# Branch gates and branch products by token instead of by channel in a two-layer fp32 block kernel

## The chip, the cores and the metric

The kernel runs on one core of a Trainium2 chip. The metric is device time in microseconds (us), the median of several executions; lower is better. Engines are TensorE (PE; its weight loads are shown apart as PEld), VectorE (DVE), ScalarE (ACT), GpSimd (POOL) and SyncE (SP), which issues the weight transfers.

## The reference

Two layers over 256 tokens of width 1024, all in float32. The change lies in the first layer's merge of three branches:

```python
h = rmsnorm(x, g_mix)
proj = h @ w_in                      # holds among others br_gate, 3 * 1024 columns
y_fox, y_sc, y_dn                    # three branches, 512 channels each
ys = jnp.stack([y_fox, y_sc, y_dn], axis=2)
gates = jax.nn.sigmoid(br_gate).reshape(bsz, seq, N_BRANCH, D_MODEL)
merged = jnp.sum(jnp.einsum('bsnc,ncd->bsnd', ys, w_branch) * gates, axis=2)
x = x + merged @ w_o
```

y_fox is an attention with forget gates, y_sc a gated short convolution, y_dn a gated delta rule in chunks of 64 tokens. A feed-forward part, and a second layer, follow; the change doesn't touch them.

## The kernel before

**Products in three parts.** Every weight matrix arrives in units of 128 x 2048 numbers (1 MB). Each unit is split in a high part (`whi`, rounded by ACT, L891, 3 slots) and a low part (`low`, by DVE, L1299, 5 slots), and the activations likewise (`hhi`, `hlo` in `hboth`; `ahi`, `alo`). A product is high x high, high x low and low x high, summed in PSUM. `mm(u, part)` issues half of unit u; part 0 ends with `half_done`, part 1 with `unit_done`.

**Kinds of units.** In C and B units the weights are stationary and 256 tokens stream past: the result has channels on the partitions. C units (1024 x 256 weights) issue 24 matmuls of 256 columns a half, in lines 2009, 2010 and 2015, and fill one bank, 4 or 5 in turn. B units (512 x 512 weights) do the same with bank 4 in part 0 and bank 5 in part 1, or banks 2g and 2g + 1 for the last branch. In T and D units the activations are stationary and 512 weight columns stream: the result has tokens on the partitions, 12 matmuls of 512 columns a half, in lines 2041, 2043 and 2056. Two T units with k0 = 0 and 4 accumulate in the same two banks, one bank per tile of 128 tokens.

**The order of the work.** One list, `order`, gives the order in which all engines walk through the steps; each engine executes its share of each step. The front has 38 units, numbered 0 to 37, so halves 0 to 75. `steps_at` puts the small steps of the attention and of the delta rule (`dn_...`) behind given halves. What reads a unit's result is held back in `held` and comes behind the next unit's part 0 (`flush`). At `mm(u, 0)` ACT makes `whi` of unit u + 2, as soon as unit u - 1 is done, and at `mm(u, 1)` DVE makes `low` of unit u + 2.

**The merge.** Units 20, 21, 23, 24, 26, 27, 29, 30 and 32 to 35 are the twelve gate units, 22, 25, 28, 31, 36 and 37 the branch units. ACT's `gate` (L1029) takes one bank through Sigmoid into `gates`; DVE's `merge` multiplies a bank of branch products with it (L1688) and, from the second branch on, adds (L1697). For the last branch ACT rounds the merged sum (L1081) and DVE takes the low part (`merge_lo`, L1706); the four w_o units (kind D, banks 0 to 3) follow, 256 rows each. Steps of the delta rule that the prediction names: `dn_tok`, `dn_decay` and `dn_kk` behind half 45, `dn_y` (level mask in L1621) behind 57, `dn_sum(0)` behind 65, `dn_sum(1)` and `dn_out(0)` behind 66, `dn_out(1)` behind 69. `dn_sum` on ACT sums squares (L879) and takes a Sqrt (L1065); `dn_out` rounds (L1075).

**Semaphores of the banks.** `c4`, `c5`, `g0` and `g1` count how often banks 4, 5, 0 and 1, and 2 and 3 were freed. A unit with `first` waits in part 0 for the first and in part 1 for the second name of its `free` list.

Of the kernel before, what the change touches and what calls it, by code (L numbers as in the profile page):

```python
# [6 lines left out]
P = 128  # L7
# [17 lines left out]
def build(nc, a, shapes, place):  # L25

    T, D = shapes["x"][1:]
    TT = T // P
# [41 lines left out]
    def unit_c(w, act, needs):  # L70
        before = [u for u in units if u["kind"] in "CB" or u.get("banks") == (4, 5)]
        bank = 5 if before and before[-1]["kind"] == "C" and before[-1]["bank"] == 4 else 4
        return add("C", w, act, needs, [f"c{bank}"], bank=bank)
# [3 lines left out]

    def unit_b(w, act, k0, needs, bank, groups):
        return add("B", w, act, needs, groups, bank=bank, k0=k0)
# [73 lines left out]
    def weave(fill, mixed):  # L153


        pending = []
        halves_ = [(u, part, then) for u, *then in fill for part in range(2)]
        scale, credit, done = len(halves_) / sum(n for n, _ in mixed), 0.0, 0

        def put(u, part, then):  # L160
            order.append(("mm", u, part))
            if part == 0 and (units[u]["kind"] == "B" or held and held[0][0] == "merge"):

                flush()
            elif part == 1 and then and then[0][0] == "merge":
                flush()
                order.append(then[0])
                held.extend(then[1:])
            elif part == 0:
                pending.append(1)  # L170
            else:
                if pending:
                    flush()
                    pending.clear()
                held.extend(then)

        if held:
            put(*halves_[0])
            flush()
            pending.clear()  # L180
            done = 1
        for n, s in mixed:
            credit += n * scale
            while credit > 0.999 and done < len(halves_):
                put(*halves_[done])
                done += 1
                credit -= 1
            order.append(s)
            if pending:
                flush()  # L190
                pending.clear()
        for h in halves_[done:]:
            put(*h)
        flush()

    def attention(which):

        for g in range(8):
            if 1 <= g < 7:
                yield (1, ("att_norm", which, g - 1))  # L200
            if g < 6:
                yield (1.0 if g else 1, ("att_scores", which, g))
            if 1 <= g < 7:
                yield (1, ("att_turn", which, g - 1))
            if g >= 2:
                yield (1.5 if g == 7 else 0, ("att_values", which, g - 2))

# [37 lines left out]
    gate_unit = {}  # L245
# [26 lines left out]
    gate(1)  # L272
    gate(0)
    branch(0, 0, "fox_lo")
    gate(2)
    gate(3)
    branch(0, 1, "fox_lo")
    gate(4)
    gate(5)
    branch(1, 0, "sc_lo")  # L280
    gate(6)
    gate(7)
    branch(1, 1, "sc_lo")
    gate(11)
    gate(10)
    gate(8)
    gate(9)
# [43 lines left out]
    for at, (u, *then) in enumerate(front):  # L331
        order.append(("mm", u, 0))
        flush()
        for s in steps_at.get(2 * at, ()):
            step(*s)
        order.append(("mm", u, 1))
        if units[u]["kind"] == "B":
            order.append(then[0])
            held.append(then[1])
        else:  # L340
            held.extend(then)
        if then and then[0][:2] == ("merge", NB - 1):
            g = then[0][2]
            if g:
                held.append(("merge_lo", 1))
            held.append(("merge_lo", 2 * g))
        for s in steps_at.get(2 * at + 1, ()):
            step(*s)
    flush()
    step("merge_lo", 3)  # L350
# [205 lines left out]
    with ctx:  # L556
# [79 lines left out]
        gates = tiles(view(3072, 6144))  # L636
# [27 lines left out]
        mg = gates[:, 0:KD, :]  # L664
# [194 lines left out]
        def _(act):  # L859
# [167 lines left out]
            def gate(e, u):  # L1027
                act.wait_ge(sem("unit_done"), u + 1)
                act.activation(gates[:, 2 * e:2 * e + 2, :], tiles(ps[:, units[u]["bank"], :]), ACT.Sigmoid)\  # L1029
                   .then_inc(took(u)[0], 1)  # L1030
# [46 lines left out]
            def merge(n_, g, b, u):  # L1077
                if n_ == NB - 1:
                    s = slice(4 * g + 2 * b, 4 * g + 2 * b + 2)
                    act.wait_ge(sem("merged"), 2 * g + b + 1)  # L1080
                    act.activation(hhi[:, s, :], mg[:, s, :], ACT.Copy).then_inc(sem("merged_hi"), 1)  # L1081
# [166 lines left out]
            def dn_unit():  # L1248
# [11 lines left out]
                         dn_sol=dn_sol, dn_out=dn_out, merge=merge, ple_gate=ple_gate, ple_p=ple_p,  # L1260
# [13 lines left out]
        def _(dve):  # L1274
# [406 lines left out]
            def merge(n_, g, b, u):  # L1681
                done = sem("half_done") if b == 0 else sem("unit_done")
                dve.wait_ge(done, u + 1)
                dve.wait_ge(*took(gate_unit[4 * n_ + 2 * g + b]))
                s = 4 * g + 2 * b
                merged = mg[:, s:s + 2, :]
                gate_ = gates[:, KD * n_ + s:KD * n_ + s + 2, :]
                ins = dve.tensor_tensor(gate_, tiles(ps[:, units[u]["bank"] + b, :]), gate_, ALU.mult)  # L1688
                if n_ < NB - 1:
                    own(ins, f"c{4 + b}", units[u]["free"][b][1] + 1)  # L1690
                elif b == 1:
# [8 lines left out]
                else:  # L1700
                    own(ins, "merged", 2 * g + b + 1)

            def merge_lo(i):
                dve.wait_ge(sem("merged_hi"), i + 1)
                s = slice(2 * i, 2 * i + 2)
                dve.tensor_tensor(hlo[:, s, :], mg[:, s, :], hhi[:, s, :].bitcast(F32), ALU.subtract)\  # L1706
                   .then_inc(sem("merged_lo"), 1)
# [169 lines left out]
            def gla_turn(b):  # L1877
# [8 lines left out]
                for t in range(TT):  # L1886
                    dve.wait_ge(sem("gla_hi"), 2 * b + t + 1)
                    for i in range(4):
# [15 lines left out]
                         dn_new=dn_new, dn_state=dn_state, dn_out=dn_out, merge=merge, merge_lo=merge_lo, resid=resid, up=up,  # L1904
# [12 lines left out]
        def _(pe):  # L1917
            def mm(u, part):
# [40 lines left out]
                if w["kind"] in "CB":  # L1959
                    nk, width = (KD, 256) if w["kind"] == "C" else (4, 512)  # L1960
# [451 lines left out]
            parts = dict(mm=mm, norm_first=norm_first, norm_wide=norm_wide, small=small, small_turn=small_turn, fox_turn=fox_turn, fox_cum=fox_cum,  # L2412
# [17 lines left out]
def laid_out(v, np):  # L2430
# [16 lines left out]
    def cut(w, *widths):  # L2447
# [8 lines left out]
        w_gate=units(gate, D, 256), w_small=by_tile(np.concatenate([f, b_a], axis=1)),  # L2456
# [52 lines left out]
```

## Time and profile before

| | |
|---|---|
| median of 3 times | 1131.43 us (1129.44 to 1131.69) |
| span of the profiled execution | 1127.7 us, 17514 instructions |
| around the span (median less span) | 3.7 us |
| PE busy | 1100.3 us, 98% |
| PE weight loads busy | 973.8 us, 86% |
| DVE busy | 767.3 us, 68% |
| ACT busy | 556.2 us, 49% |
| mean granted TensorE clock | 0.993 |

Busy time of PE is pipelined time: its ends are modelled, so the distance from one start to the next is what counts. The profiled execution has no time of its own beside its span; the times come from other executions.

### The profile page before, as it was taken

The page shows a single profiled execution, that of the slowest core. Times are in us where ns is not written, and L with a number is a line of the kernel's source. Part 1 is how long each engine was busy: PE and PEld are TensorE (multiplying, and loading weights), DVE is VectorE, ACT ScalarE, POOL GpSimd, SP SyncE. Part 2 cuts the span into 40 slices and gives each one's busy share as a digit, 9 for nine tenths or more (in the row PEclk, how much of TensorE's full clock was granted, in tenths as well). Part 3 has the DMA queues.
Part 4 walks back from the last instruction along what each step waited for, and adds up shares of the span by engine and source line. Part 5 has one row for each costly group of instructions (what it writes and reads, how often), then busy time and mean ns, then how long its engine had stood idle before and what let it go on. Part 6 is the DMA issues. An engine that isn't in the chain of part 4 may idle for free.

```text
span 1127.7 us, 17514 instructions
## 1 busy us (share of the span) xinstructions
PE 1100.3 (98%) x7442; PEld 973.8 (86%) x7442; DVE 767.3 (68%) x937; ACT 556.2 (49%) x664; POOL 36.4 (3%) x98
## 2 busy tenths in 40 slices
PE   9989999999999999999998999999999999999997
PEld 8888998997989999998797888888888888888886
DVE  5486788554668998787677575556667866656555
ACT  6466564333535443445665454444455665444443
POOL 6000000000000000000003200000000000000000
PEclk9998999999999999999999999999999999999999
DMA  8542443333355555554453355555534435555551
GB/s 306 181 156 75 150 150 116 111 116 110 130 175 194 187 187 187 187 187 167 169 180 134 129 174 190 194 196 198 191 119 174 153 115 187 184 190 187 187 187 56
DMA packets 27455, 185.07 MB, mean 164 GB/s; under 512 B 3169, under 2 KB 3681, under 8 KB 5618
## 3 DMA queue, kind: packets, MB, share of 16 engines
q1 hardware_dynamic: 26208, 182.46, 45.9%
q10 hardware_dynamic: 1170, 1.49, 0.4%
q8 instruction: 59, 0.97, 0.3%
q14 instruction: 18, 0.15, 0.1%
HBM read 182.89 MB, written 1.05 MB: 163 GB/s over the span
## 4 chain that ended last, share of the span: by engine, by line
PE 89%; DVE 7%; ACT 2%; issue 1%; POOL 0%; DVEq 0%; ACTq 0%; POOLq 0%
PE ps L2041 12%; PE ps L2056 12%; PE ps L2043 12%; PE ps L1971 10%; PE ps L2009 9%; PE ps L2015 9%; PE ps L2010 9%; PE ps L1977 5%; DVE low L1299 2%; DVE arena L1466 1%; PE ps L2073 1%; PE ps L1991 1%; PE ps L2375 1%; PE ps L2237 1%; PE ps L2143 0%
## 5 line engine op out<-in xcount | busy, mean ns | idle before, releaser
L891 ACT ACTIVATE whi<-raw 128x2048 fp32r<-128x2048 f32 x170 | 324.3, 1913 | 333.1 <-PE ps L2056 165.8
L1299 DVE TENSOR_TENSOR low<-raw,whi 128x2048 fp32r<-128x2048 f32 x170 | 389.2, 2293 | 40.3 <-ACT whi L891 37.4
L2009 PE MATMUL ps<-hboth,whi 128*128 128x256 f32 x880 | 221.0, 289 | 3.3 <-ACT conv L980 3.3
L2010 PE MATMUL ps<-hboth,whi 128*128 128x256 f32 x880 | 217.0, 284 | 0.0
L2009 PEld LDWEIGHTS ps<-hboth,whi 128*128 128x128 f32 x880 | 169.4, 192 | 7.9 <-ACT whi L891 3.6
L2010 PEld LDWEIGHTS ps<-hboth,whi 128*128 128x128 f32 x880 | 169.7, 193 | 0.7 <-issue 0.2
L2041 PE MATMUL ps<-whi,ahi 128*128 128x512 f32 x416 | 164.2, 395 | 2.8 <-issue 1.9
L2043 PE MATMUL ps<-whi,alo 128*128 128x512 f32 x416 | 162.8, 391 | 0.0
L1971 PE MATMUL ps<-hboth,whi 128*128 128x512 f32 x512 | 128.1, 392 | 0.0
L2015 PE MATMUL ps<-hboth,low 128*128 128x256 f32 x880 | 124.2, 284 | 0.5 <-DVE low L1299 0.5
L2056 PE MATMUL ps<-low,ahi 128*128 128x512 f32 x416 | 119.7, 389 | 0.0
L2015 PEld LDWEIGHTS ps<-hboth,low 128*128 128x128 f32 x880 | 114.3, 193 | 0.7 <-DVE low L1299 0.7
L1971 PEld LDWEIGHTS ps<-hboth,whi 128*128 128x128 f32 x512 | 93.7, 188 | 18.5 <-issue 0.7
L2041 PEld LDWEIGHTS ps<-whi,ahi 128*128 128x128 f32 x416 | 78.6, 189 | 18.8 <-issue 4.0
L2056 PEld LDWEIGHTS ps<-low,ahi 128*128 128x128 f32 x416 | 78.1, 188 | 16.4
L2043 PEld LDWEIGHTS ps<-whi,alo 128*128 128x128 f32 x416 | 78.6, 189 | 14.9
L1977 PEld LDWEIGHTS ps<-hboth,low 128*128 128x128 f32 x512 | 69.8, 190 | 5.0
L2041 PE MATMUL ps<-whi,hboth 128*128 128x512 f32 x186 | 73.7, 396 | 0.0
L2043 PE MATMUL ps<-whi,hboth 128*128 128x512 f32 x186 | 72.5, 390 | 0.0
L1977 PE MATMUL ps<-hboth,low 128*128 128x256 f32 x512 | 71.4, 282 | 0.0
L1801 DVE TENSOR_TENSOR cy<-cy,ps 128x512 f32<-128x512 f32 x32 | 22.0, 687 | 70.0 <-ACT cy L1149 70.0
L1808 DVE TENSOR_TENSOR alo<-cy,ahi 128x512 fp32r<-128x512 f32 x32 | 22.2, 692 | 51.7 <-ACT ahi L1156 51.7
(376 smaller groups left out, 1216.1 us busy)
## 6 DMA issues: line engine op xcount, KB each, us to landing
raw<-in_ffn_up SPq DMA_DIRECT2D x32, 1024.0 KB, 4.8
raw<-in_ffn_down SPq DMA_DIRECT2D x32, 1024.0 KB, 4.9
raw<-in_w_up SPq DMA_DIRECT2D x22, 1024.0 KB, 4.9
raw<-in_w_gate SPq DMA_DIRECT2D x12, 1024.0 KB, 4.9
raw<-in_w_down SPq DMA_DIRECT2D x11, 1024.0 KB, 4.9
raw<-in_w_dn SPq DMA_DIRECT2D x6, 1024.0 KB, 4.9
raw<-in_w_sc SPq DMA_DIRECT2D x6, 1024.0 KB, 4.8
raw<-in_w_branch SPq DMA_DIRECT2D x6, 1024.0 KB, 4.8
```

What stands on the lines that cost most here:

```text
L891: act.activation(whi[:, u % SPLIT, :], raw[:, u % RAW, :], ACT.Copy).then_inc(sem("hi_done"), 1)
L1299: dve.tensor_tensor(wlo[:, u % RAW, :], raw[:, u % RAW, :], whi[:, u % SPLIT, :].bitcast(F32), ALU.subtract).then_inc(sem("lo_done"), 1)
L1801: own(dve.tensor_tensor(y, y, both[:, :, 0, :], ALU.add), *took_name(u))
L1808: dve.tensor_tensor(alo[:, s, :], cy[:, i % 2, :, :], ahi[:, s, :].bitcast(F32), ALU.subtract)\
L1971: pe.matmul(out, whi[:, s, at:at + P], hboth[:, k, :, :].rearrange("p a t -> p (a t)"), start=k == 0, stop=False, skip_group_check=True)
L1977: ins = pe.matmul(ps[:, w["bank"] + ct, 0:T], low[:, at:at + P], hhi[:, k, :], start=False, stop=k == KD - 1, skip_group_check=True)
L2009: pe.matmul(out, wh, hi[:, k0 + k, :], start=opens and k == 0, stop=False, skip_group_check=True)
L2010: pe.matmul(out, wh, lo[:, k0 + k, :], start=False, stop=False, skip_group_check=True)
L2015: ins = pe.matmul(out, low[:, at:at + P], hi[:, k0 + k, :], start=False, stop=k == nk - 1, skip_group_check=True)
L2041: pe.matmul(ps[:, bank, :], hi[:, k0 + k, part * P:(part + 1) * P], wh, start=w["first"] and k == 0, stop=False, skip_group_check=True)
L2043: pe.matmul(ps[:, bank, :], lo[:, k0 + k, part * P:(part + 1) * P], wh, start=False, stop=False, skip_group_check=True)
L2056: ins = pe.matmul(ps[:, bank, :], hi[:, k0 + k, part * P:(part + 1) * P], low[:, at:at + 512], start=False, stop=w["last"] and k == nk - 1 ...
```

## The change

The twelve gate units become T units of 512 x 512 weights, two (k0 = 0 and 4) for each pair of branch n and half g of the 1024 channels; the six branch units become T units too. Gates, branch products and the merged sum so have tokens on the partitions. A gate's Sigmoid is issued right behind its second unit, no longer held back, once for each tile of 128 tokens. `merge` keeps its place and its operations. The merged sum is transposed on PE in 16 pieces of 128 x 128 (`merge_turn`) into banks 4 to 7, from where ACT rounds and DVE takes the low part; `merge_turn(0)` stands ahead of the first w_o unit, `merge_turn(1)` behind it. Gates 8 to 11 come in the order (2, 1), (2, 0).

```diff
     def branch(n, g, need):
-        bank, groups = (4, ["c4", "c5"]) if n < NB - 1 else (2 * g, [f"g{g}"])
-        u = unit_b(a["w_branch"][2 * n + g], "a", BT * n, [(need, 2)], bank, groups)
+        banks, groups = ((4, 5), ["c4", "c5"]) if n < NB - 1 else ((2 * g, 2 * g + 1), [f"g{g}"])
+        u = add("T", a["w_branch"][2 * n + g], "a", [(need, 2)], groups, banks=banks, k0=BT * n, first=True, last=True)
         front.append((u, ("merge", n, g, 0, u), ("merge", n, g, 1, u)))
...
-    def gate(e):
-        u = unit_c(a["w_gate"][e], "h", h_ready)
-        gate_unit[e] = u
-        front.append((u, ("gate", e, u)))
+    def gate(n, g):
+        for half in range(2):
+            u = unit_t(a["w_gate"][2 * NB * half + 2 * n + g], half)
+            front.append((u,) if half == 0 else (u, ("gate", n, g, 0, u), ("gate", n, g, 1, u)))
+        gate_freed[n, g] = [after("c4"), after("c5")]
...
-    gate(11)
-    gate(10)
-    gate(8)
-    gate(9)
+    gate(2, 1)
+    gate(2, 0)
     branch(2, 0, "dn_lo")
     branch(2, 1, "dn_lo")
...
         order.append(("mm", u, 1))
-        if units[u]["kind"] == "B":
+        if then and then[0][0] == "gate":
+            order.extend(then)
+        elif then and then[0][0] == "merge":
             order.append(then[0])
             held.append(then[1])
...
+        if then and then[0] == ("merge", NB - 1, 1, 0, u):
+            step("merge_turn", 0)
     us = [unit_d(a["w_o"][i], "h", 2 * i, i == 0, i == 3, [("merged_lo", i + 1)]) for i in range(4)]
-    for u in us[:3]:
+    product(us[0])
+    step("merge_turn", 1)
+    for u in us[1:3]:
         product(u)
...
+            def gate(n_, g, t, u):
+                act.wait_ge(sem("half_done") if t == 0 else sem("unit_done"), u + 1)
+                act.activation(gates[:, n_, t, 512 * g:512 * (g + 1)], ps[:, 4 + t, :], ACT.Sigmoid)\
+                   .then_inc(sem(gate_freed[n_, g][t][0]), 1)
...
+            def merge_turn(g):
+                for pair in (2 * g, 2 * g + 1):
+                    act.wait_ge(sem("merge_turned"), pair + 1)
+                    act.activation(hhi[:, 2 * pair:2 * pair + 2, :], tiles(ps[:, 4 + pair, :]), ACT.Copy)\
+                       .then_inc(sem("merged_hi"), 1)
...
+            def merge_turn(g):
+                for pair in (2 * g, 2 * g + 1):
+                    dve.wait_ge(sem("merged_hi"), pair + 1)
+                    s = slice(2 * pair, 2 * pair + 2)
+                    dve.tensor_tensor(hlo[:, s, :], tiles(ps[:, 4 + pair, :]), hhi[:, s, :].bitcast(F32), ALU.subtract)\
+                       .then_inc(sem("merged_lo"), 1)
...
+            def merge_turn(g):
+                pe.wait_ge(sem("merged"), 2 * (g + 1))
+                for pair in (2 * g, 2 * g + 1):
+                    for k in (2 * pair, 2 * pair + 1):
+                        for t in range(TT):
+                            at = (k % 2) * T + t * P
+                            ins = pe.transpose(ps[:, 4 + pair, at:at + P], mg[:, t, k * P:(k + 1) * P], ident[:, :])
+                    ins.then_inc(sem("merge_turned"), 1)
...
-        w_gate=units(gate, D, 256), w_small=by_tile(np.concatenate([f, b_a], axis=1)),
+        w_gate=units(gate, 512, 512), w_small=by_tile(np.concatenate([f, b_a], axis=1)),
```

## Rows read from the trace of the kernel before

**Rows 1.** The page: busy time by engine, and the chain's shares.

```profile
PE 1100.3 (98%) x7442; PEld 973.8 (86%) x7442; DVE 767.3 (68%) x937; ACT 556.2 (49%) x664; POOL 36.4 (3%) x98
...
PE 89%; DVE 7%; ACT 2%; issue 1%; POOL 0%; DVEq 0%; ACTq 0%; POOLq 0%
```

**Rows 2.** Chain, last branch halves and first w_o: start us, us, what.

```profile
300.70 0.96 PE ps L2015 x8
...
312.22 0.96 PE ps L2015 x8
313.18 0.23 PE ps L2041
```

**Rows 3.** Chain, fox units at the kernel's start.

```profile
16.07 0.91 PE ps L2056 x4
...
35.11 0.91 PE ps L2056 x4
```

**Rows 4.** Windows: stretch, length, busy by engine (instructions), clock, DMA share, GB/s.

```profile
16.07:37.83 21.76, 21.76 (x98) 18.02 (x97) 11.73 (x10) 11.14 (x10) 6.14 (x28) 1.00 0.68 250
...
296.00:313.00 17.00, 17.00 (x144) 17.00 (x143) 13.58 (x13) 8.27 (x8) 0.00 (x0) 1.00 0.53 186
```

**Rows 5.** Timeline of PE: first and ninth or seventeenth matmul after a step.

```profile
278.11 0.39 PE L2009 MATMUL ps<-hboth,whi 128*128 128x256 f32 x1
...
280.13 1.12 PE L2015 MATMUL ps<-hboth,low 128*128 128x256 f32 x8
...
871.29 0.50 PE L2041 MATMUL ps<-whi,hboth 128*128 128x512 f32 x1
...
873.24 1.07 PE L2056 MATMUL ps<-low,hboth 128*128 128x512 f32 x4
```

**Rows 6.** Timeline of PE and DVE around half 46.

```profile
183.07 0.39 PE L2009 MATMUL ps<-hboth,whi 128*128 128x256 f32 x1
...
186.91 0.68 DVE L1688 TENSOR_TENSOR arena<-ps,arena 128x512 f32<-128x512 f32 x1
```

**Rows 7.** Timeline of ACT, DVE and PE around halves 56 and 57.

```profile
224.90 1.92 ACT L891 ACTIVATE whi<-raw 128x2048 fp32r<-128x2048 f32 x1 [4.83 <-PE ps L2015]
...
230.50 0.42 DVE L1621 TENSOR_TENSOR arena<-arena,packs 128x256 f32<-128x256 f32 x1
...
231.29 0.68 PE L2237 MATMUL ps<-arena 64*64 64x64 f32 x16
```

**Rows 8.** Timeline of ACT, and PE's half 67, from half 64 to 68.

```profile
275.61 0.60 ACT L1029 ACTIVATE arena<-ps 128x512 f32<-128x512 f32 x1
286.18 0.28 ACT L879 ACTIVATE cy<-ps 128x128 f32<-128x128 f32 x1 [9.97 <-PE ps L2294]
...
287.34 1.28 ACT L1065 ACT_TABLE_LOAD   x1
...
291.18 0.63 ACT L1075 ACTIVATE ahi<-arena 128x512 fp32r<-128x512 f32 x1 [1.70 <-DVE arena L1674]
...
286.48 0.36 PE L2009 MATMUL ps<-hboth,whi 128*128 128x256 f32 x1
```

**Rows 9.** Groups of ACT, table loads: busy us, mean ns, idle before.

```profile
L1029 ACT ACT_TABLE_LOAD x4 | 5.1, 1283 | 0.1
L1065 ACT ACT_TABLE_LOAD x2 | 2.6, 1283 | 0.0
```

**Rows 10.** Timeline of PE: eight transposes and the half after them.

```profile
164.80 1.03 PE L2194 MATMUL ps<-ident,arena 128*128 128x128 f32 x8
165.59 0.36 PE L2009 MATMUL ps<-hboth,whi 128*128 128x256 f32 x1
```

**Rows 11.** Waits of PE, 0 to 335 us: us, times, longest.

```profile
PE ps L2293 <- DVE arena L1644: 1.8, 2, 0.9
...
PE ps L2280 <- DVE xs L1653: 0.8, 1, 0.8
```

More of the change, by code:

```diff
@@ L70, in unit_c @@
     def unit_c(w, act, needs):
-        before = [u for u in units if u["kind"] in "CB" or u.get("banks") == (4, 5)]
+        before = [u for u in units if u["kind"] == "C" or u.get("banks") == (4, 5)]
         bank = 5 if before and before[-1]["kind"] == "C" and before[-1]["bank"] == 4 else 4
@@ L76, in unit_w @@
         return add("C", w, act, needs, ["c4" if bank == 4 else "c5"], bank=bank, wide=True)
-    def unit_b(w, act, k0, needs, bank, groups):
-        return add("B", w, act, needs, groups, bank=bank, k0=k0)
     def unit_t(w, half):
@@ L151, in flush @@
         held.clear()
[L153 to L206, printed above, removed]
     step("first_root", 0)
@@ L271, in build @@
     sc(1, 0)
-    gate(1)
-    gate(0)
+    gate(0, 0)
     branch(0, 0, "fox_lo")
-    gate(2)
-    gate(3)
+    gate(0, 1)
     branch(0, 1, "fox_lo")
-    gate(4)
-    gate(5)
+    gate(1, 0)
     branch(1, 0, "sc_lo")
-    gate(6)
-    gate(7)
+    gate(1, 1)
     branch(1, 1, "sc_lo")
-    gate(11)
-    gate(10)
-    gate(8)
-    gate(9)
+    gate(2, 1)
+    gate(2, 0)
     branch(2, 0, "dn_lo")
@@ L635, in build @@
         kcT = dnT[:, 2 * DH:3 * DH, :]
-        gates = tiles(view(3072, 6144))
+        gates = view(3072, 3 * TT * D).rearrange("p (n t d) -> p n t d", n=NB, t=TT)
         fqkv = view(3072, 3072).rearrange("p (t n) -> p t n", t=TT)
@@ L663, in build @@
         EG = [by(xs[:, 1, 512:1024], DH), S]
-        mg = gates[:, 0:KD, :]
+        mg = gates[:, 0]
         idle = flat[1][:, 0:P]
@@ L1025, in z @@
                    .then_inc(took(u)[0], 1)
[L1027 to L1030, printed above, removed]
+            def gate(n_, g, t, u):
+                act.wait_ge(sem("half_done") if t == 0 else sem("unit_done"), u + 1)
+                act.activation(gates[:, n_, t, 512 * g:512 * (g + 1)], ps[:, 4 + t, :], ACT.Sigmoid)\
+                   .then_inc(sem(gate_freed[n_, g][t][0]), 1)
             def dn_cum():
@@ L1259, in _ @@
                          gate=gate, dn_cum=dn_cum, dn_decay=dn_decay, dn_x0=dn_x0, dn_y=dn_y,
-                         dn_sol=dn_sol, dn_out=dn_out, merge=merge, ple_gate=ple_gate, ple_p=ple_p,
+                         dn_sol=dn_sol, dn_out=dn_out, merge_turn=merge_turn, ple_gate=ple_gate, ple_p=ple_p,
                          ab_qk=ab_qk, ab_v=ab_v, lam=lam, pool_mm=pool_mm,
@@ L1679, in dn_out, with merge @@
                 own(dve.tensor_tensor(alo[s], dnout, ahi[s].bitcast(F32), ALU.subtract), "dn_lo", t + 1)
[L1681 to L1688, printed above, removed]
+            def merge(n_, g, t, u):
+                dve.wait_ge(sem("half_done") if t == 0 else sem("unit_done"), u + 1)
+                dve.wait_ge(sem(gate_freed[n_, g][t][0]), gate_freed[n_, g][t][1])
+                s = slice(512 * g, 512 * (g + 1))
+                merged, gate_ = mg[:, t, s], gates[:, n_, t, s]
+                ins = dve.tensor_tensor(gate_, ps[:, units[u]["banks"][t], :], gate_, ALU.mult)
                 if n_ < NB - 1:
-                    own(ins, f"c{4 + b}", units[u]["free"][b][1] + 1)
-                elif b == 1:
+                    own(ins, f"c{4 + t}", units[u]["free"][t][1] + 1)
+                elif t == 1:
                     own(ins, f"g{g}", units[u]["free"][0][1] + 1)
@@ L1700, in merge @@
                 else:
[L1701 to L1707, printed above, removed]
+                    own(ins, "merged", 2 * g + t + 1)
+            def merge_turn(g):
[4 more added lines that the diff above has]
+                       .then_inc(sem("merged_lo"), 1)
             def added(xt, banks, t, u):
@@ L1903, in _ @@
                          dn_pre=dn_pre, dn_decay=dn_decay, dn_kk=dn_kk, dn_x0=dn_x0, dn_y=dn_y, dn_z=dn_z, dn_sol=dn_sol,
-                         dn_new=dn_new, dn_state=dn_state, dn_out=dn_out, merge=merge, merge_lo=merge_lo, resid=resid, up=up,
+                         dn_new=dn_new, dn_state=dn_state, dn_out=dn_out, merge=merge, merge_turn=merge_turn, resid=resid, up=up,
                          ple_p=ple_p, ple_x=ple_x, lam=lam, pool_mm=pool_mm,
@@ L1957, in rounded @@
                     pe.wait_ge(sem("norm_hi"), KD * fresh[u] + k + 1)
-                if w["kind"] in "CB":
-                    nk, width = (KD, 256) if w["kind"] == "C" else (4, 512)
+                if w["kind"] == "C":
+                    nk, width = KD, 256
                     n = width // P // 2
```

16 lines of the change are left out of this document (2 added, 14 removed).

## The prediction

> **What bounds the kernel now.** I read the page first: TensorE (PE) is busy 98% of the span and the chain that ended last runs through it for 89% [rows 1]. So the question in the stage that changes is how long PE's own list of instructions is, and where it would have to wait. I number the 38 units of the front 0 to 37 and their halves 0 to 75; the change touches halves 40 to 75 (24 gate halves, 12 branch halves), from 157.8 us to the first product with w_o at about 313 us. Next I read the chain there: halves follow each other without a gap. At the end four halves of 24 matmuls of 256 columns take (312.22 - 300.70) / 4 = 2.88 us each, 0.120 us a matmul [rows 2]. Halves of 12 matmuls of 512 columns, in the fox units at the kernel's start, take (35.11 - 16.07) / 7 = 2.72 us, 0.227 us a matmul [rows 3]. The windows say why: with 256 columns the weight loads fill the whole stretch (PEld 17.00 of 17.00 us), with 512 they don't (18.02 of 21.76), and the granted clock is 1.00 (2.4 GHz) in both [rows 4]. Streaming 512 columns takes less than two matmuls of 256.
>
> **The stream.** 36 halves get shorter by 0.16 us: -5.8 us. Columns and DMA bytes stay the same. Some 18 of these halves come after a step of the delta rule. The first eight pairs there cost 2.02 us instead of 1.92 with 256 columns, and eight matmuls of 512 cost 1.95 instead of 1.82 [rows 5]: about 0.03 us more for the new form at each re-entry, +0.6 us.
>
> **The waits for banks.** This is the part that costs. A C unit filled one bank, 4 or 5 in turn, and its reader had a whole unit's time. A gate is now two T units that write bank 4 in part 0 and bank 5 in part 1, so each bank must be free one half earlier, and two gates in a row use the same two banks. I walked the 36 halves through the queues of ACT and DVE; ACT and DVE execute in the order of the list. Three places bind.
>
> Half 47 (unit 23, part 1, bank 5). Bank 5 was read by merge(0, 0, 1), which in DVE's queue lies behind the steps of half 45. Its multiplication ran from 186.91 to 187.60, while PE began half 46 at 183.07 [rows 6]. Before, half 47 went on in bank 4. Now it could start at 183.07 + 2.85 = 185.9 and waits to 187.65: +1.7 us. Behind it in PE's queue is only dn_kk 1, late by the same.
>
> Half 57 (the steps after it). The sigmoid of gate(1, 0, 1) now comes right after its own unit, ahead of the split of unit 30's weights on ACT (1.92 us at 224.90). All behind it moves by about 0.5 us: split, low part on DVE, the two merge instructions, and then the level mask at 230.50 + 0.42, which PE needs at 231.29 [rows 7]. PE arrives 0.3 us earlier than before, since halves 56 and 57 are shorter. Slack was 0.3; +0.45 us.
>
> Half 68 (unit 34, part 0, bank 4). Gate(2, 0) follows gate(2, 1) without a branch between, in the same banks. Its first half needs the sigmoid of gate(2, 1, 0). That stands in ACT's list behind the steps of half 66: dn_sum(1) and dn_out(0). These wait for the last state on PE; the sums end at 287.3, a Sqrt table load and the roots follow, DVE's 1/root, scaling and product, and ACT's rounding at 291.18 to 291.81 [rows 8]. Before, a sigmoid ran between the two dn_sum, at 275.61, and its table load put the second Sqrt load of 1.28 us into the chain [rows 8, 9]. With the change no sigmoid is there, so one Sqrt load falls away and the chain ends 1.28 us sooner: 290.55. Then come the Sigmoid load (1.28) and the sigmoid (0.59): bank 4 is free at 292.5. PE is there at 286.48 + 2.85 = 289.35: +3.15 us. Queued behind on PE are all nine halves and w_o; on ACT the split of unit 36 is 2.5 us later, with a unit in hand. Halves 69 to 75 find their inputs: bank 5 is free at 293.1 for half 69 at 295.3; half 69 ends at 298.0, dn_out(1) takes four transposes (0.4), and three instructions of about 0.7 on DVE, ACT and DVE finish the branch's last input at about 300.7, for half 72 at 304.
>
> The rest of the walk has slack of 0.6 us or more: half 65 needs bank 5 from merge(1, 1, 1), which DVE ends some 0.6 us before; gates free banks 4 and 5 for the branch units within 0.6 us of a half's or unit's end, the third unit's weights lie ready, and RAW = 5 keeps DMA ahead. DVE's arithmetic is the same 20 instructions of 512 columns; its and ACT's four copies and subtractions stay four, only out of PSUM.
>
> The Trainium skill, page Perfetto Trace Analysis, section Optimizing Tensor Performance, speaks against the change: matmul groups should rotate through different PSUM banks, so that one's evacuation lies under the next one's matmuls; it grants as well that larger matmuls are more efficient. By its first half a wait is due at every pair of gates; the walk finds it where no branch or step lies between, and at half 47.
>
> **The transposes.** 16 new transposes. Eight of this shape cost 0.79 us (164.80 to 165.59) [rows 10]. The first eight stand between the last branch half and w_o. The path: the first four are issued in 0.4 us and complete 0.24 later, as the eight do (1.03 against 0.79) [rows 10]; ACT's copy of 512 columns takes 0.60 [rows 8], DVE's subtraction 0.69, as its other operations of 512 columns [rows 6], and I add 0.15 for the hand-overs. So w_o's first half starts 2.1 us after the last branch half; before, it started at once (312.22 + 0.96 = 313.18) [rows 2]. In my walk DVE is done with merge(2, 1, 0) by then. +2.1 us. The second eight go between the first and second w_o units, whose operands are ready: +0.8, and 0.1 for re-entry. Merge(2, 1, 1), which frees banks 2 and 3 and gates these transposes, ends 1.3 us after w_o's part 0 began, with 2.7 available.
>
> **Sum.** -5.8 + 0.6 + 1.7 + 0.45 + 3.15 + 2.1 + 0.9 = +3.1 us. The profiled execution has a span of 1127.7 us; the median of the three times is 1131.43, 3.7 us lie outside the span. 1131.4 + 3.1 = 1134.5 us.
>
> **Bounds.** T halves: from 0.16 down to 0.06 us saved (if the pitch were that of matmuls after a re-entry, 0.235) [rows 5]. Half 47: 0 to 1.9. Half 68: without the saved Sqrt load 4.4; nothing, if the sigmoid got done in time. Turn: 0.8 (copies hidden) to 2.7 (DVE late by one multiply and add). Bounds of single terms seldom add up; the range takes about half of their sum on either side.
>
> **The rivals.** (a) Not slower: half 68 doesn't wait, because ACT would reach the first sigmoid before PE finishes half 67. For it: ACT is busy 49% of the span and idle for most of 276 to 286 [rows 1, 8]. Against it: the sigmoid's input is complete only after half 66, at 281, and in the list it comes behind dn_sum(1), which waited for PE to 286.1 (9.97 us idle) [rows 8]. Sum: 0.0, 1131.4 us. It decides as soon as the wait is below 2.3 us. 0.17, together with smaller waits that lead to the same sum.
> (b) Slower still by ACT: the second Sqrt load stays, or other table loads enter; and the delta rule's ping-pong between PE, ACT and DVE, late by the sigmoids now ahead of it, gives further waits of 0.1 to 0.3 us in the six steps. +1.3 to +2.5: 1136 to 1137 us. 0.20.
> (c) The stream gains little: 0.06 us a half, -2.2 instead of -5.8: 1138 us. Every long run of rows stands against it. 0.05.
> The Trainium skill, page TensorE: Matmul & The Clock Gate, section Back-to-back issue gap, gives an isolated gap of N / 2.4 + 2.5 ns; by it a half would save only 0.03 us and the sum would be about +7.8 us. The rows, 0.120 and 0.227, disagree with it.
> (d) Faster: no bank wait costs PE time, as PE would have been held by the delta rule's steps anyway, and only the turn remains: -5.8 + 0.6 + 3.0 = -2.2, 1129.2 us, just at the edge. For it: PE did wait in some steps of the delta rule, 0.9 and 0.8 us at a time [rows 11]. Against it: all of these waits come to 2.6 us, and none lies at half 47 or 68. 0.08.
> The forecast: 0.50.
>
> **How the numbers follow.** A change of 0.2% (2.3 us) is about what a measurement of this kernel can tell from none. Slower: most of the forecast, all of (b) and (c), 0.65. Same: (a), the lower edge of the forecast, half of (d): 0.27. Faster: 0.08. The range from 1131.2 to 1137.3 leaves out (c), most of (d) and some of (a) below it.
>
> **What would show it.** Right: L2041/L2043/L2056 halves of 2.72 us from 158 to 315 us; PE waits on DVE at about 187, on ACT's sigmoid at about 290 (3 us); Sigmoid loads three, Sqrt load one at dn_sum; a gap of some 1.2 us after eight transposes before w_o. Wrong: no wait at half 68, or waits at other halves I took for covered, such as 65 or 72; T halves of other length in this stage.

## The result, and the profile after

The changed kernel takes 1135.68 us (median of 11 times, 1131.72 to 1137.57), the kernel before 1129.61 us beside it on the same chip (11 times). The ratio of the two sets is 1.0046, with an interval of 1.0032 to 1.0060: slower by 5.2 us (the two medians lie 6.1 apart), where +3.1 was forecast. The profiled execution took 1136.17 us, 1.8 of them outside its span of 1134.4.

The page of the changed kernel: busy time by engine, and the chain's shares by engine. It answers to [rows 1].

```profile
PE 1100.2 (97%) x7026; PEld 951.9 (84%) x7026; DVE 768.2 (68%) x937; ACT 553.7 (49%) x662; POOL 36.5 (3%) x98
...
PE 86%; DVE 8%; issue 3%; ACT 3%; POOL 0%; DVEq 0%; ACTq 0%; POOLq 0%
```

There are 416 fewer matmuls, yet PE is busy as long as before in a longer span, and 3% of the chain have left it for "issue", DVE and ACT. Where, the waits of PE in the first 345 us say (engine, line, what it waited for, us in total, times, longest):

```profile
PE ps L1976 <- ACT arena L965: 3.1, 1, 3.1
...
PE ps L1976 <- DVE arena L1622: 1.6, 1, 1.6
...
PE ps L1976 <- issue: 1.1, 1, 1.1
...
PE ps L2181 <- DVE arena L1557: 0.3, 1, 0.3
```

Before, no row of the list named a sigmoid, a merge or the turn. Lines have moved: L1976, L1978 and L1991 are the matmuls of T and D units (L2041, L2043 and L2056 before), L965 the sigmoid, L1622 the merge's product, L1557 the level mask, L1001 the Sqrt of `dn_sum`, L1011 the rounding of `dn_out`, L2018 the new transposes, L1016 and L1641 ACT's and DVE's part of `merge_turn`.

Next the timeline of PE at the waits (start us, us, engine, line, operation; in brackets the idle time before and who ended it):

```profile
181.33 0.50 PE L1976 MATMUL ps<-whi,hboth 128*128 128x512 f32 x1
...
185.90 0.50 PE L1976 MATMUL ps<-whi,hboth 128*128 128x512 f32 x1 [1.56 <-DVE arena L1622]
...
188.87 1.15 PE L2160 MATMUL ps<-arena 128*64 128x64 f32 x32
...
220.58 0.50 PE L1976 MATMUL ps<-whi,hboth 128*128 128x512 f32 x1
...
226.25 0.68 PE L2181 MATMUL ps<-arena,cy 64*64 64x64 f32 x16
226.86 0.50 PE L1976 MATMUL ps<-whi,ahi 128*128 128x512 f32 x1
...
228.81 1.07 PE L1991 MATMUL ps<-low,ahi 128*128 128x512 f32 x4
...
230.20 0.68 PE L2181 MATMUL ps<-arena 64*64 64x64 f32 x16 [0.33 <-DVE arena L1557]
...
287.37 0.48 PE L1976 MATMUL ps<-whi,hboth 128*128 128x512 f32 x1
...
293.47 0.47 PE L1976 MATMUL ps<-whi,hboth 128*128 128x512 f32 x1 [3.09 <-ACT arena L965]
...
308.35 1.07 PE L1991 MATMUL ps<-low,ahi 128*128 128x512 f32 x4
...
316.51 1.07 PE L1991 MATMUL ps<-low,ahi 128*128 128x512 f32 x4
317.42 1.03 PE L2018 MATMUL ps<-ident,arena 128*128 128x128 f32 x8
319.55 0.47 PE L1976 MATMUL ps<-whi,hboth 128*128 128x512 f32 x1 [1.09 <-issue]
...
325.12 1.03 PE L2018 MATMUL ps<-ident,arena 128*128 128x128 f32 x8
325.91 0.48 PE L1976 MATMUL ps<-whi,hboth 128*128 128x512 f32 x1
```

Three halves apart, the last branch halves are (316.51 - 308.35) / 3 = 2.72 us each, against 2.88 [rows 2]. The eight first matmuls after a step cost 228.81 - 226.86 = 1.95 us, as the other T units did [rows 5]. Halves 46 and 47, from 181.33 to the step at 188.87, take 7.54 us, where halves 54 and 55 without a wait take 226.25 - 220.58 = 5.67: the wait at half 47 costs 1.87. A bracket shows less than a wait costs, since PE's records end later than their last issue and the first matmuls behind a wait are slow again: four matmuls that are issued in 0.91 us have a record of 1.07 (316.51 to 317.42), and the first behind the wait takes 0.34 us to the next instead of 0.227.

ACT's timeline from the last sums to the sigmoid that half 68 waits for answers to [rows 8]:

```profile
288.24 0.85 ACT L1001 ACTIVATE ss<-ss,dnr 128x1 f32<-128x1 f32 x4
290.79 0.63 ACT L1011 ACTIVATE ahi<-arena 128x512 fp32r<-128x512 f32 x1 [1.70 <-DVE arena L1610]
291.44 1.28 ACT L965 ACT_TABLE_LOAD   x1
292.73 1.09 ACT L965 ACTIVATE arena<-ps 128x512 f32<-128x512 f32 x2
```

The four roots come without a table load ahead of them, then the Sigmoid load of 1.28 us and the two sigmoids, and PE starts half 68 when the first of these is done. The groups of ACT's table loads from 150 to 320 us (busy us, mean ns, idle before) are one fewer each than in [rows 9], as forecast:

```profile
L965 ACT ACT_TABLE_LOAD x3 | 3.8, 1283 | 0.1
...
L1001 ACT ACT_TABLE_LOAD x1 | 1.3, 1283 | 0.0
```

What was not forecast stands in the windows (stretch, length, busy by engine, then the granted clock, DMA share, GB/s). The last row is the whole stage, from half 40 to the transposes of the norm behind w_o.

```profile
268.00:274.00 6.00, 5.14 (x29) 3.44 (x28) 3.13 (x4) 1.91 (x1) 0.00 (x0) 1.00 0.49 161
...
274.50:281.50 7.00, 7.00 (x22) 5.39 (x21) 1.12 (x4) 0.00 (x0) 0.00 (x0) 0.52 0.00 0
...
295.00:297.80 2.80, 2.80 (x8) 2.23 (x7) 2.15 (x1) 0.62 (x1) 0.00 (x0) 0.50 0.00 0
...
156.84:341.10 184.26, 174.98 (x1306) 137.38 (x1304) 106.16 (x135) 71.12 (x91) 0.00 (x0) 0.97 0.37 126
```

The same windows of the kernel before, its stage and a stretch ahead of it:

```profile
157.75:333.56 175.81, 172.56 (x1721) 157.07 (x1720) 106.03 (x135) 73.89 (x93) 0.00 (x0) 1.00 0.38 132
...
108.00:112.00 4.00, 4.00 (x21) 4.00 (x19) 2.38 (x7) 2.72 (x3) 0.00 (x0) 0.50 0.00 0
```

The stage grew by 8.45 us, from 175.81 to 184.26. Twice the granted clock fell to half, 1.2 GHz, and PE was fully busy for as long as it stayed there. I call such a stretch a lapse. The first, from about 274.5 to 282, cost about 3.1 us: half 64 starts 1.8 us earlier than before and half 67 0.9 later, where three halves should have gained another 0.4. The second, from 295, cost about 1.6 by the same count. What PE did before them: ahead of the first it waited 0.86 us for a step of the delta rule, up to 272.08 (the 5.14 busy of 6.00 us in the row of 268 to 274), 2.3 us before the clock fell. The kernel before has the same wait, up to 274.17, and no lapse behind it. The second begins 1.5 us behind the wait of 3.09 us. Lapses happen in the kernel before as well (108 to 112 us above), but not in its stage. Without the two, the stage grew by 8.45 - 3.1 - 1.6 = 3.7 us.

### The profile page after: what moved, and what is told of

Read it like the earlier page. It is cut to its first block, busy times and chain, and to the rows that moved or that the text cites. A ratio compares the mean times of both kernels' runs of the same rounds, so it can differ in the third digit from the quotient of the medians.

```text
span 1134.4 us, 16681 instructions
## 1 busy us (share of the span) xinstructions
PE 1100.2 (97%) x7026; PEld 951.9 (84%) x7026; DVE 768.2 (68%) x937; ACT 553.7 (49%) x662; POOL 36.5 (3%) x98
## 4 chain that ended last, share of the span: by engine, by line
PE 86%; DVE 8%; issue 3%; ACT 3%; POOL 0%; DVEq 0%; ACTq 0%; POOLq 0%
PE ps L1976 14%; PE ps L1991 14%; PE ps L1978 14%; PE ps L1906 10%; PE ps L1944 6%; PE ps L1945 6%; PE ps L1950 6%; PE ps L1912 5%; DVE low L1235 2%; PE ps L2008 1%; PE ps L1926 1%; ACT whi L827 0%; PE ps L2238 0%; PE ps L2319 0%; PE ps L2181 0%
## 5 line engine op out<-in xcount | busy, mean ns | idle before, releaser
L1976 PE MATMUL ps<-whi,ahi 128*128 128x512 f32 x464 | 182.6, 393 | 3.5 <-issue 2.6
L1978 PE MATMUL ps<-whi,alo 128*128 128x512 f32 x464 | 181.3, 391 | 0.0
L1944 PE MATMUL ps<-hboth,whi 128*128 128x256 f32 x688 | 173.1, 289 | 3.4 <-ACT conv L916 3.3
L1945 PE MATMUL ps<-hboth,whi 128*128 128x256 f32 x688 | 170.8, 285 | 0.0
L1944 PEld LDWEIGHTS ps<-hboth,whi 128*128 128x128 f32 x688 | 133.2, 194 | 7.1 <-ACT whi L827 3.6
L1945 PEld LDWEIGHTS ps<-hboth,whi 128*128 128x128 f32 x688 | 133.5, 194 | 0.7 <-issue 0.2
L1991 PE MATMUL ps<-low,ahi 128*128 128x512 f32 x464 | 132.5, 389 | 0.0
L1976 PE MATMUL ps<-whi,hboth 128*128 128x512 f32 x282 | 114.7, 407 | 5.7 <-ACT arena L965 3.1
L1978 PE MATMUL ps<-whi,hboth 128*128 128x512 f32 x282 | 111.5, 396 | 0.0
L1906 PEld LDWEIGHTS ps<-hboth,whi 128*128 128x128 f32 x512 | 93.7, 188 | 18.5 <-issue 0.7
L1976 PEld LDWEIGHTS ps<-whi,ahi 128*128 128x128 f32 x464 | 87.3, 188 | 21.5 <-issue 4.9
L1991 PEld LDWEIGHTS ps<-low,ahi 128*128 128x128 f32 x464 | 87.1, 188 | 18.2
L1978 PEld LDWEIGHTS ps<-whi,alo 128*128 128x128 f32 x464 | 87.3, 188 | 16.8
L1950 PE MATMUL ps<-hboth,low 128*128 128x256 f32 x688 | 97.2, 284 | 0.0
L1950 PEld LDWEIGHTS ps<-hboth,low 128*128 128x128 f32 x688 | 89.6, 194 | 0.0
L1991 PE MATMUL ps<-low,hboth 128*128 128x512 f32 x288 | 80.1, 393 | 0.0
L1912 PEld LDWEIGHTS ps<-hboth,low 128*128 128x128 f32 x512 | 69.8, 190 | 5.0
L1912 PE MATMUL ps<-hboth,low 128*128 128x256 f32 x512 | 71.4, 282 | 0.0
L1976 PEld LDWEIGHTS ps<-whi,hboth 128*128 128x128 f32 x282 | 53.7, 191 | 19.0 <-issue 5.5
```

The lines of the kernel that those rows point to most:

```text
L1906: pe.matmul(out, whi[:, s, at:at + P], hboth[:, k, :, :].rearrange("p a t -> p (a t)"), start=k == 0, stop=False, skip_group_check=True)
L1912: ins = pe.matmul(ps[:, w["bank"] + ct, 0:T], low[:, at:at + P], hhi[:, k, :], start=False, stop=k == KD - 1, skip_group_check=True)
L1944: pe.matmul(out, wh, hi[:, k0 + k, :], start=opens and k == 0, stop=False, skip_group_check=True)
L1945: pe.matmul(out, wh, lo[:, k0 + k, :], start=False, stop=False, skip_group_check=True)
L1950: ins = pe.matmul(out, low[:, at:at + P], hi[:, k0 + k, :], start=False, stop=k == nk - 1, skip_group_check=True)
L1976: pe.matmul(ps[:, bank, :], hi[:, k0 + k, part * P:(part + 1) * P], wh, start=w["first"] and k == 0, stop=False, skip_group_check=True)
```

## The experiments

For 154 executions, of all kernels here, there are a time and a mean granted clock. I fitted them with one offset for each kernel and one slope for all: the slope is 0.71 (0.03) us for each 0.001 of mean clock, and 0.66 us remain. In brackets I give standard errors. "At equal clock" below is a kernel's offset from the kernel before by this fit. The kernel before ran at a mean clock of 0.9941 (65 runs), the changed one at 0.9922 (19 runs). An offset at equal clock leaves out what a kernel loses by a lower clock of its own, so it is no forecast of its time.

| kernel | median us (n) | ratio to before, interval | clock | at equal clock, us |
|---|---|---|---|---|
| changed, once more (the last two columns with both sets) | 1134.89 (8) | 1.0037 [1.0023, 1.0051] | 0.9922 | +4.0 (0.2) |
| sum_later | 1133.24 (12) | 1.0032 [1.0021, 1.0042] | 0.9929 | +3.1 (0.2) |
| merge_now | 1132.51 (11) | 1.0031 [1.0018, 1.0045] | 0.9919 | +1.9 (0.2) |
| t0_early | 1132.91 (7) | 1.0029 [1.0018, 1.0039] | 0.9936 | +2.5 (0.3) |
| all_three | 1131.00 (12) | 1.0006 [0.9997, 1.0015] | 0.9940 | +1.2 (0.2) |
| best | 1129.08 (11) | 1.0001 [0.9993, 1.0010] | 0.9932 | -0.9 (0.2) |
| before_wait | 1131.83 (12) | 1.0018 [1.0009, 1.0027] | 0.9937 | +2.3 (0.2) |
| three_waits | 1139.48 (5) | 1.0093 [1.0077, 1.0109] | 0.9912 | +8.1 (0.3) |

The kernel before beside these took 1129.38 us (31 runs), 1129.24 (24) and 1129.34 (9).

**after_again: the changed kernel once more.**

> The changed kernel once more, unchanged, beside the others on one chip. Theory A (fixed waits plus stream: about +3.5 us) and in addition a lower TensorE clock in one or two stretches of the front that comes and goes by itself: time +3 to +6 us over the kernel before, from execution to execution as the mean granted clock lies at 0.996 to 0.989. Theory B (the wait at half 68 pulls the clock down each time): a stretch at 1.2 GHz within 3 us behind half 68's start in the profile again, and time +5 us or more.

1134.89 us, ratio 1.0037, a loss of 4.2 us by the ratio and of 5.5 by the medians. The loss stands: with both sets of runs it is +4.0 us at equal clock, and its clock is lower by 0.0019, which at 0.71 us for 0.001 is another 1.35. The second profile has two lapses in the stage again, from about 256.6 and from 290.8 us; its stage took 183.90 us. In the windows:

```profile
256.00:260.00 4.00, 3.72 (x13) 3.01 (x14) 2.18 (x3) 0.00 (x0) 0.00 (x0) 0.58 0.00 0
...
288.00:292.00 4.00, 0.90 (x4) 0.51 (x3) 3.20 (x4) 2.95 (x5) 0.00 (x0) 0.85 0.57 180
```

The first begins 0.3 us behind a wait of 0.79 us in the delta rule. The second begins while PE is idle in half 68's wait of 3.1 us (288.6 to 291.8), and goes on for 6 us behind it. So the sign that theory B named, a stretch at 1.2 GHz close behind half 68's start, is there in both profiles; merge_now below has the same wait and no lapse, so it isn't there each time.

**sum_later: two steps of the delta rule move one half back**, so that ACT comes to the sigmoids of gate(2, 1) first.

```diff
-        66: [("dn_new", 3), ("dn_state", 3), ("dn_sum", 1), ("dn_out", 0)],
+        66: [("dn_new", 3), ("dn_state", 3)],
+        67: [("dn_sum", 1), ("dn_out", 0)],
```

> dn_sum(1) and dn_out(0) stand behind half 67 and behind the two sigmoids of gate(2, 1), instead of behind half 66. If the wait at half 68 (3.09 us in the trace) comes from the sigmoid's place in ACT's list, it is gone, nothing takes its place (half 72's input is ready 3 us early), and the kernel is 3.1 us faster than the changed one: about +0.5 us over the kernel before by the mechanics alone, +2 with the clock. If the wait also pulls the clock down behind it (theory B), the gain is 4.5 to 5 us. Rival: PE waits for dn_out(1) at half 69's end instead, 1 us or more, and the gain is 2 or less.

The waits of PE in the stage:

```profile
PE ps L1977 <- ACT whi L828: 2.6, 1, 2.6
...
PE ps L1977 <- DVE arena L1623: 1.6, 1, 1.6
...
PE ps L1977 <- issue: 0.7, 1, 0.7
```

The wait at half 68 is gone, so that its cause was the place in ACT's list. That nothing would take its place was wrong. But `dn_out` is now late, half 72 waits 0.7 us for the branch's input, and DVE comes with a backlog to the last merges: the first w_o half waits 2.65 us instead of 1.09. Of 3.1 us only 0.9 come back at equal clock (-3.1 + 0.7 + 1.6 = -0.8 by the trace). The name ACT whi L828 on the longest row is misleading: this is w_o's half, and the last of its inputs to be written was DVE's low part of the turned sum, at 314.86 + 0.69 us, with PE's start at 315.65.

**merge_now: merge(0, 0, 1) right behind half 45**, ahead of the steps, so bank 5 is free for half 47.

```diff
-            held.append(then[1])
+            (order if then[0][1:3] == (0, 0) else held).append(then[1])
```

> The changed kernel with one step moved: merge(0, 0, 1) stands right behind half 45 instead of behind half 46. If half 47's wait (1.56 us in the trace) comes from DVE's order, it is gone, DVE's steps of the delta rule behind it lose nothing (its 0.69 us lie under PE's first transposes), and the kernel is 1.6 us faster than the changed one at the same clock. Rival: dn_decay's chain gets later by 0.3 to 0.7 us and takes half of it back.

At equal clock this takes away 2.2 us (4.02 to 1.85, each with an error of 0.2), where the trace gives 1.87. The row of the wait on L1622 is gone, the others stay. In its profile the stage had no lapse at all:

```profile
160.49:338.26 177.77, 170.03 (x1305) 134.07 (x1303) 106.05 (x135) 71.12 (x91) 0.00 (x0) 1.00 0.38 131
```

With the 1.87 us put back this is 179.64, or 3.8 us above 175.81: the fixed part of the loss, in a stage with the clock at 1.00. Its mean clock is low all the same (0.990 in this execution, 0.9919 over all): the lapses of this profile lie outside the stage, from about 7, 82, 106 and 621 us.

**t0_early: the first sigmoid of gate(2, 1) ahead of the steps of half 66**, the second stays where it is.

```diff
+        if at == 33:
+            order.append(then[0])
         for s in steps_at.get(2 * at, ()):
             step(*s)
         order.append(("mm", u, 1))
         if then and then[0][0] == "gate":
-            order.extend(then)
+            order.extend(then[1:] if at == 33 else then)
```

> The changed kernel with one step moved: the sigmoid of gate(2, 1, 0) stands right behind half 66, ahead of dn_sum(1). Bank 4 is free long before half 68. But the Sigmoid load comes between the two dn_sum again, so the second Sqrt load (1.28 us) is back in the chain and bank 5 (the sigmoid of gate(2, 1, 1)) is free only about 1.3 us later than in the changed kernel. Expected: four Sigmoid loads, two Sqrt loads, no wait at half 68, a wait of some 1.7 us at half 69 in its place, 1.4 us less than the changed kernel. The rival, by which table loads cost nothing here, expects a wait of 0.4 us at half 69 and 2.7 us less.

The timeline at PE's half 69:

```profile
293.16 0.50 PE L1978 MATMUL ps<-whi,hboth 128*128 128x512 f32 x1 [1.58 <-ACT arena L967]
```

and ACT's table loads:

```profile
L967 ACT ACT_TABLE_LOAD x4 | 5.1, 1283 | 0.1
...
L1003 ACT ACT_TABLE_LOAD x2 | 2.6, 1283 | 0.0
```

Half 68 runs without a wait, half 69 waits 1.58 us for the second sigmoid, and both table loads are back. 1.5 us are won at equal clock, as the difference of the waits (3.09 - 1.58) says. So the table loads belong to this chain, and the sigmoid between the two `dn_sum` brings the second Sqrt load, as read from [rows 8, 9].

**all_three: both moves, and merge_turn(0) between the halves of the last branch unit**, ahead of `mm(u, 1)`.

```diff
         for s in steps_at.get(2 * at, ()):
             step(*s)
+        if then and then[0] == ("merge", NB - 1, 1, 0, u):
+            step("merge_turn", 0)
         order.append(("mm", u, 1))
...
-        if then and then[0] == ("merge", NB - 1, 1, 0, u):
-            step("merge_turn", 0)
```

(with the edits of sum_later and merge_now)

> Three repairs of the order: dn_sum(1) and dn_out(0) behind half 67; merge(0, 0, 1) right behind half 45; the first eight transposes between the halves of the last branch unit. The theory of fixed waits expects -3.1, -1.6 and -1.1 us against the changed kernel, so about 2 us (0.2%) faster than the kernel before if the clock is the same. The rival, that the stream itself gains less than 5 us, expects it equal to the kernel before or slower.

The waits of PE in the stage (L2019 are the new transposes):

```profile
PE ps L2019 <- DVE arena L1632: 1.8, 1, 1.8
...
PE ps L1977 <- issue: 0.7, 1, 0.7
PE ps L1977 <- DVE arena L1623: 0.4, 1, 0.4
```

5.8 us were expected back, 2.9 came. The transposes between the halves now wait 1.8 us themselves, for the end of merge(2, 0) on DVE: before that DVE stood idle for 1.84 us, from 303.36 to 305.21, until ACT had split a unit's weights. The copies are hidden, but what they need is not ready sooner.

**best: merge_turn also gets its inputs in time.** For the last branch the first merge of a unit stands between its halves, and the second sigmoid of gate(1, 0) is held back again, so that half 57's level mask comes as before.

```diff
-        order.append(("mm", u, 1))
-        if then and then[0][0] == "gate":
-            order.extend(then)
+        last = then and then[0][:2] == ("merge", NB - 1)
+        if last:
+            order.append(then[0])
+            if then[0][2] == 1:
+                step("merge_turn", 0)
+        order.append(("mm", u, 1))
+        if last:
+            held.append(then[1])
+        elif then and then[0][0] == "gate":
+            order.append(then[0])
+            (held if then[0][1:3] == (1, 0) else order).append(then[1])
```

(with the edits of sum_later and merge_now)

> The three repairs of the order, and two more: the first merge of each of the last two branch units stands ahead of the low part that DVE makes at the same unit (DVE stood idle for 1.8 us before it), and the second sigmoid of gate(1, 0) is held back as it was in the kernel before. Expected at the transposes 0.4 us of waiting instead of 1.8, none at w_o, none behind half 57: about 2 us less than with the three repairs alone, 1129.0 us, and with the clock of the kernel before 0.1 to 0.2% faster than that. The rival, that the gain of the stream is used up by chance of the clock, expects no difference that can be told from the kernel before.

The waits of PE in the stage that the kernel before has not, and the windows of the stage and of a stretch in it:

```profile
PE ps L1983 <- issue: 0.7, 1, 0.7
...
PE ps L2025 <- DVE arena L1638: 0.4, 1, 0.4
```

```profile
157.91:333.83 175.92, 171.55 (x1305) 135.09 (x1303) 105.84 (x135) 73.81 (x93) 0.00 (x0) 0.99 0.38 132
256.00:260.00 4.00, 4.00 (x14) 3.06 (x13) 2.93 (x2) 0.00 (x0) 0.00 (x0) 0.59 0.00 0
```

The waits at halves 47, 57 and 68 and at w_o are gone, and 0.7 and 0.4 us remain. The stage takes 175.92 us, as before, with one lapse in it that cost 1.57 us by the lengths of its units; without that, 1.5 us less than before. The time is 1129.08 us, where 1129.0 was expected, ratio 1.0001: equal to the kernel before, and 0.9 us better at equal clock. But its mean clock is lower than that of the kernel before, by 0.0009 (error 0.0003), though the long waits are gone. So what the stream gains at full clock doesn't show in the times, and that part of the lower clock belongs to the new form of the products, and not to waits, isn't ruled out.

**before_wait: the kernel before, with half 68's wait alone.** The form of the products and the transposes are left as they were; PE waits at half 68 for `dn_out(0)`.

```diff
+                if u == 34 and first:
+                    pe.wait_ge(sem("dn_hi"), 1)
```

> The kernel before, with one wait added on PE: half 68 waits for the rounding of dn_out(0) on ACT, which ended at 291.81 us where half 68 began at 289.4. If a wait costs what it lasts, +2.4 us. If such a wait at this place pulls the clock down behind it (theory B), +4 us or more, and the profile shows a stretch at 1.2 GHz from about 294 us.

The added wait, and a window just ahead of it:

```profile
PE ps L2011 <- ACT ahi L1075: 1.4, 1, 1.4
```

```profile
284.00:288.00 4.00, 4.00 (x20) 3.10 (x19) 0.00 (x0) 2.27 (x9) 0.00 (x0) 0.57 0.00 0
```

+2.3 us at equal clock, and the clock, 0.9937 against 0.9941, hardly lower. In the profile the bracket is only 1.4 us, since a lapse ahead of it, from 284 to 288, had made PE late for it. One wait of some 2.4 us costs its own length; that it brings a lapse with it each time was not shown.

**three_waits: the kernel before, with all three waits.** To the wait of before_wait come one in half 47 for merge(0, 0, 1), and one at the first w_o half for the second low part.

```diff
+                if u == 23 and not first:
+                    pe.wait_ge(sem("c5"), units[22]["free"][1][1] + 1)
+                if u == 38 and first:
+                    pe.wait_ge(sem("merged_lo"), 2)
```

> The kernel before, C and B units and all, with three waits on PE at the places of the changed kernel: half 47 until merge(0, 0, 1) has freed bank 5 (about 1.7 us), half 68 until ACT has rounded dn_out(0) (2.4 us), the first w_o product until its second input (2.4 us). If a wait costs what it lasts: +6.5 us at equal clock. If the waits are also what lowers the mean granted clock of the changed kernel (0.9922 against 0.9941 over all executions so far), the mean lies at 0.992 here too and the time is +7.5 to +8. If the form of the matmuls does that (512 columns, half as many weight loads), the mean clock stays at 0.994 and the time at +6.5 or less.

The three waits, and two windows, one about as long as the stage and one of a stretch in it:

```profile
PE ps L2047 <- DVE hboth L1706: 2.7, 1, 2.7
...
PE ps L2015 <- ACT ahi L1075: 2.5, 1, 2.5
...
PE ps L2015 <- DVE arena L1688: 1.4, 1, 1.4
```

```profile
156.00:344.00 188.00, 178.13 (x1729) 161.91 (x1728) 106.72 (x135) 73.88 (x93) 0.00 (x0) 0.97 0.35 123
...
280.00:284.00 4.00, 4.00 (x19) 3.78 (x19) 1.12 (x4) 0.00 (x0) 0.00 (x0) 0.50 0.00 0
```

The brackets add up to 6.6 us (2.7 + 2.5 + 1.4), and perhaps 7.4 with the re-entry and the hidden part of each, 0.28 as at half 47 (0.13 of it re-entry). The median rises by 10.1 (ratio 1.0093): 8.1 at equal clock (0.3), of which some 0.7 have no wait to stand for them, and 2.1 by a mean clock of 0.9912 (error 0.0007; the 9 runs of the kernel before beside it have 0.9940). The stage itself runs from 157.03 to 344.55, 187.5 us, with two lapses, from 277.7 us and from 322.1, the second within the wait ahead of w_o. The old form of the products, with waits alone, so shows the low clock that the changed kernel shows. These are five runs, but the ratio's lower end, 1.0077, is a loss of 8.7 us and excludes both sums.

**before_again: the kernel before, a second profile.**

> The kernel before, for a second profile of it. If stretches at 1.2 GHz between 250 and 320 us belong to the changed kernel alone, there is none here; if they come by chance in any kernel's delta rule, there may be one.

The window of its stage:

```profile
160.40:336.24 175.84, 172.59 (x1722) 157.09 (x1720) 106.10 (x135) 73.88 (x93) 0.00 (x0) 1.00 0.38 132
```

The stage without a lapse again, in 175.84 us, though this execution had three lapses ahead of it (from about 7, 82 and 106 us) and took 1131.16 us.

## Why the prediction was right in its direction and off in its size

The terms of the sum, in us; the measured terms are differences between starts on PE, with the clock at 1.00.

| term | forecast | measured | from |
|---|---|---|---|
| stream with re-entry | -5.2 | -5.0 | 18 halves x 0.16, 18 behind a step x 0.12 |
| half 47 | +1.7 | +1.9 | 7.54 - 5.67 |
| half 57 | +0.45 | +0.4 | 230.20 - 226.86 = 3.34, less 2.95 (211.98 - 209.03) for a half without the wait |
| half 68 | +3.15 | +3.4 | 293.47 - (287.37 + 2.86) = 3.24, and 0.13 for re-entry |
| turn before w_o | +2.1 | +2.3 | 319.55 - 317.42, and 0.13 |
| second eight transposes | +0.9 | +0.9 | 325.91 - 325.12, and 0.12 |
| sum | +3.1 | +3.8 | 3.7 by the stage, 3.8 by merge_now, 4.0 (0.2) by the fit |
| lower mean clock | 0 | +1.35 | 0.0019 x 0.71 / 0.001 |
| all | +3.1 | +5.2 | 1.0046; 4.2 by the second set's ratio, 5.4 by the means of all runs |

- **The stream** was right: 2.72 us a half, from the fox units' rows [rows 3]. A half behind a step saves 0.12 and not 0.13, and rival (c) falls.
- **The waits for banks** were right in place, cause and price. merge_now moves one place in a list and takes away the wait at half 47 alone; sum_later and t0_early move the other and take away the one at half 68. Rival (a), no wait at half 68, falls. The Trainium skill's rule that independent matmul groups should rotate through PSUM banks (Perfetto Trace Analysis, Optimizing Tensor Performance) agrees with the traces at halves 47 and 68. What made the waits is the reader's place: the bank's reader was ready to run, but stood behind other work in its engine's list.
- **The chain with the table loads** was right: three Sigmoid loads and one Sqrt load, and the roots straight behind the sums. Rival (b) named table loads and the delta rule's steps as the way to a larger loss. Its size above the kernel before, +4.4 to +5.6 (forecast and its +1.3 to +2.5), covers the 5.2 that were measured, but by another cause: no extra load appeared and no step waits longer than in [rows 11].
- **The turn** was right: ACT's copies and DVE's subtraction follow at the forecast distance, the bracket is 1.09 us against a gap of 1.2.
- **Luck in the absolute time.** The forecast of 1134.5 us misses 1135.68 by only 1.2. It was added to 1131.43, the median of three executions; eleven of the kernel before gave 1129.61. A base that was 1.8 too high so hid most of a sum that was 2.1 too low.
- **The steps that failed.** The smaller one: each place where PE stops costs a re-entry of 0.13 us behind it. The prediction charged it for the steps and the second eight transposes, not behind half 47, half 68 and the turn, and put the stream 0.2 too high; together +0.7. The larger one: the sum took the granted clock as 1.00 throughout, since [rows 4] showed 1.00, and added every wait at its own length. The changed kernel runs with a mean clock lower by 0.0019 (error 0.0005), worth 1.35 us.
- **Shown of the clock, and not shown.** That waits alone can lower it is shown by three_waits, which has none of the new products. That one wait does is not: before_wait's clock is lower by 0.0004, the size of its error. Nor can the fall be split over the three waits, or between waits and the new form: best, without the long waits, is still 0.0009 lower. Lapses in the stage were in both profiles of the changed kernel, in four of its five variants' and in both with added waits, and in neither of the kernel before. All twelve of them begin within an idle stretch of PE of 0.78 us or more, or at most 2.5 us behind the end of one. The kernel before has three such stretches in its stage, all in the delta rule (0.78, 0.86 and 0.94 us), the changed one six. So more waits give more places for a lapse; this is a count over eleven profiles and not an experiment. Not each place brings one: of 51 such stretches 39 had none, among them merge_now's wait of 3.1 us at half 68. And the lapse from 255.7 to 256.9 us, behind the same wait of 0.78 us that the kernel before has, is in five of seven profiles with the new products and in none of four with the old ones. Which stretch brings a lapse is open, and with it what of the 1.35 us the form of the products has a part in.
- **The rival on the faster side**, (d), was right that a kernel with the waits gone gains: best's stage is 1.5 us shorter at full clock. It was wrong that this one would have none.

## What to carry to other kernels

When banks are reused sooner, look up where the bank's reader stands in its own engine's list: a reader behind unrelated small steps makes TensorE wait for all of them. Taking one such wait away may only pass it on (sum_later, all_three); place the reader, what it reads, and what feeds that together, and add up again. And for a kernel that keeps TensorE busy 98% of the time, expect that new waits can cost more than their length: here three of 6.6 us together cost 10.1, through a re-entry behind each, a lower mean clock, and some 0.7 us that stay unexplained, while a single one of about 2.4 us cost 2.3 at equal clock.

## What the runs showed of the hardware

- The granted clock falls to half, 1.2 GHz, for some 3 to 7 us at a time. In the stage of the merge each such lapse begins within an idle stretch of TensorE or up to 2.5 us behind one, be it as short as 0.78 us (best, where it ends at 255.4 us and the lapse begins at 255.8). Another begins between 105 and 107 us in all eleven profiles, and there TensorE had been busy for at least 3.5 us before. Some lapses move between executions of the same kernel: the second profile of the kernel before has them from 7 and 82 us, the first has neither. Of the kernel before's executions the one of 1127.35 us had a mean clock of 0.997, the one of 1133.39 us 0.989: 6.0 us apart, of which the slope explains 8 x 0.71 = 5.7.
- A table load of 1283 ns was followed by the sigmoid at once (291.44 + 1.28 = 292.72, start at 292.73). The Trainium skill (ScalarE: Activation LUTs, What ACT_TABLE_LOAD costs) gives the same 1283 ns, and about 1380 ns of a drain on top; no such gap is in these rows, and the measurement decides.
